# RWKV-7 rounds reordered: four-quarter products, sums with the identity on GpSimd

## The chip, the cores and the metric

The kernel runs on one core of a Trainium2 chip. The metric is the device time of one execution in microseconds (us); lower is better. TensorE (PE) multiplies into PSUM banks; VectorE (DVE), ScalarE (ACT) and GpSimd (POOL) work on SBUF tiles of 128 partitions; semaphores order them.

## The reference, cut to what matters

Two layers of a hybrid backbone over 256 context and 256 latent tokens. The change touches one mixer of layer 1, the bidirectional RWKV-7 with 16 heads of 64:

```python
def rwkv7_scan(r, w, k, v, a, b, state):
    def step(S, inp):
        r_t, w_t, k_t, v_t, a_t, b_t = inp
        sa = jnp.einsum('bhvk,bhk->bhv', S, a_t)
        S = S * w_t[:, :, None, :] + sa[..., None] * b_t[:, :, None, :] + v_t[..., None] * k_t[:, :, None, :]
        return S, jnp.einsum('bhvk,bhk->bhv', S, r_t)
...
        w_log = -jax.nn.softplus(-(rw_w0[d] + jnp.tanh(w_low[..., d, :]) @ rw_w2[d])) - 0.5
        a = jax.nn.sigmoid(rw_a0[d] + a_low[..., d, :] @ rw_a2[d])
        k_d = k * (1 + (a - 1) * rw_ka)
        out.append((r, exp(-exp(w_log)), k_d, v, -kk, kk * a))
```

It runs forward and backward (d = 0, 1), first over the context, then over the latent tokens.

## The kernel before, in words

The scan is done in chunks of L = 64 tokens, four of the context (seg 0, state only) and four of the latent tokens (seg 1, with outputs Y), both directions at once. `rwkv_chunks` makes nine calls of `rwkv_round(n, main, front)`: round n does the main part of chunk n-1 and the front part of chunk n. Each of TensorE, ACT, DVE and GpSimd has its own order, written out by hand in `pe_round`, `act_round`, `dve_round` and `pool_round`; a queue runs strictly in that order and waits on labels (`at_`, `at_last`).

Front: z (decay) and za (rate) by `low_rank`; `squashed` makes sigmoids of them by eight tanh and a rescale; `scan_decay` on DVE sums the decays; `decays` on ACT makes exponentials; from these come a, b, k, r of the next chunk, the products with ka, kk and k on GpSimd. Main: X = b'a is masked to D (inside blocks of 16 tokens) and, from Xt = a'b, to Dt and Ot (between blocks); T = (1+D)(1+D2)(1+D4)(1+D8) is built by adding a power times T to T on DVE (`add_power`); N = Ot T; U = (1 + N + N N + N N N) V1 is found by three steps V2, V3, U, each with a product and a sum on DVE (`substituted`). S is the state, S' = decay (S + bt U + kt vt).

A product of 64x64 matrices takes, for 8 head pairs p, halves hf and directions d, 32 matmuls of 64 rows by 64 columns. Tiles hold one head of a pair in partitions 0 to 63 and the other in 64 to 127. `half` says in which: tiles listed in `natural` are laid out alike for both directions, others with the halves exchanged for d = 1. A matmul whose input rows and output rows are both natural or both exchanged lies on the same quarter of the array for (d, hf) = (0, 0) and (1, 1) or its neighbour; with one natural and one exchanged the four positions are four different quarters. Before, products of two exchanged tiles are done one direction after the other (`each`); `both_wide` and `each_wide` take two right sides at once, into a pair of banks. Every product takes a PSUM bank out of four a direction, in turn, and waits until the bank's last user has read it (`bank_free`).

In the trace all products of one helper have one line: L2561 single products (`head`), L2579 and L2587 double width, L2602 turned tiles, L2610 z and za; L2744 ACT's copies, L2752 its tanh, L2739 other ACT steps; L379, L382 and L385 DVE multiply, add and subtract; L2922, L2923, L2926 and L2927 GpSimd.

## Time and profile before

| | |
|---|---|
| median of 3 runs | 2333.25 us (2330.16 to 2334.47) |
| profiled execution, span | 2316.3 us |
| changed stage (rounds 1 to 8) in it | 1447.0 to 1847.4 us |
| TensorE busy, whole span | 1964.1 us (85%) |
| DVE, ACT, GpSimd busy | 941.6, 702.3, 330.4 us |

The profile is of one execution; its span leaves out what lies before the first and behind the last instruction. "Busy" counts instructions of an engine, overlapping ones once; "issue" as the reason of an idle stretch means that the profile shows nothing for which the engine waited.

### The profile page before, as it was taken

How to read it: one execution, taken by the hardware profiler on the slowest of the kernel's cores; microseconds unless marked ns; L12 is line 12 of the kernel's file. 1: busy time of each engine (PE TensorE's matmuls, PEld its weight loads, DVE VectorE, ACT ScalarE, POOL GpSimd, SP SyncE). 2: the span in 40 equal slices, each digit the busy share in tenths (PEclk: the TensorE clock that was granted, in tenths of full speed). 3: DMA queues.
4: the chain of work that ended last, by engine and by line, in shares of the span. 5: the costliest groups of instructions: out<-in, count | busy, mean ns of one | idle time of the engine just before them, and what ended most of it. 6: DMA issues, size and time to landing. Idle time of an engine off the chain costs nothing. (4 is left out here: it accounts for less than half of the span.)

```text
span 2316.3 us, 58391 instructions
## 1 busy us (share of the span) xinstructions
PE 1964.1 (85%) x26021; PEld 1364.9 (59%) x26021; DVE 941.6 (41%) x1675; ACT 702.3 (30%) x1525; POOL 330.4 (14%) x211
## 2 busy tenths in 40 slices
PE   6999998997979888998487895888888897977775
PEld 3777765445844445555253685888878755633443
DVE  3183235785051111111434577666777453111112
ACT  3234534674230000100214344455444212000001
POOL 1433310002401000000110345212311000000000
PEclk8999999998989989999799997999999977988888
DMA  8554533204265789777530220000000025899975
GB/s 298 189 204 146 183 144 146 74 1 145 73 258 217 280 302 349 277 272 285 212 111 1 70 77 28 4 5 5 4 4 4 31 91 206 301 387 365 358 295 182
DMA packets 133329, 381.14 MB, mean 165 GB/s; under 512 B 14394, under 2 KB 43670, under 8 KB 115926
## 3 DMA queue, kind: packets, MB, share of 16 engines
q1 hardware_dynamic: 114528, 343.82, 40.3%
q10 hardware_dynamic: 15094, 20.99, 3.0%
q0 software_dynamic: 3456, 12.58, 1.4%
q8 instruction: 205, 3.36, 0.6%
q14 instruction: 46, 0.38, 0.0%
HBM read 634.54 MB, written 25.95 MB: 285 GB/s over the span
## 5 line engine op out<-in xcount | busy, mean ns | idle before, releaser
L371 PE MATMUL banks<-parts 128*128 128x512 f32 (+1 forms) x1096 | 244.7, 375 | 14.5 <-POOL parts L1523 7.6
L1814 PE MATMUL banks<-arena 128*32 128x256 f32 x1696 | 218.4, 403 | 40.8 <-DMA arena<-in_exp_w_up_dram 40.8
L371 PEld LDWEIGHTS banks<-parts 128*128 128x128 f32 x1096 | 194.6, 192 | 55.2 <-POOL parts L2388 9.4
L1815 PE MATMUL banks<-arena 128*32 128x256 f32 x1696 | 218.3, 402 | 0.0
L2561 PE MATMUL banks<-arena 64*64 64x64 f32 x4224 | 159.4, 225 | 47.7 <-DVE arena L382 18.5
L1880 ACT ACTIVATE arena<-banks 64x256 f32<-64x256 f32 x78 | 29.6, 380 | 549.9 <-PE banks L1815 382.6
L2561 PEld LDWEIGHTS banks<-arena 64*64 64x64 f32 x4224 | 147.7, 140 | 52.3 <-DVE arena L382 19.9
L1814 PEld LDWEIGHTS banks<-arena 128*32 128x32 f32 x1696 | 102.0, 115 | 120.5 <-DMA arena<-in_exp_w_up_dram 44.0
L371 PE MATMUL banks<-arena,ring 128*128 128x256 f32 (+2 forms) x560 | 163.3, 459 | 9.4 <-PEq L318 8.5
L2561 PE MATMUL banks<-ring 64*64 64x64 f32 x4224 | 159.9, 225 | 8.6 <-issue 7.4
L379 DVE TENSOR_TENSOR arena<-banks,arena 64x256 f32<-64x256 f32 (+3 forms) x128 | 65.5, 511 | 241.5 <-ACT arena L1880 149.9
L2005 DVE COPY arena<-banks 128x256 f32<-128x256 f32 x78 | 33.1, 425 | 309.1 <-DMA y_sorted<-arena 226.5
L2561 PEld LDWEIGHTS banks<-ring 64*64 64x64 f32 x4224 | 147.6, 139 | 10.3 <-issue 9.3
L1836 PE MATMUL banks<-arena 128*32 128x256 f32 x1696 | 114.5, 416 | 35.7 <-DVE arena L1995 18.4
L371 PEld LDWEIGHTS banks<-arena,ring 128*128 128x128 f32 (+1 forms) x560 | 108.7, 199 | 60.4 <-issue 46.8
L371 PE MATMUL banks<-h_parts,parts_z 128*128 128x512 f32 x416 | 132.0, 397 | 3.9 <-PEq L318 3.9
L2061 POOL DMA_INDIRECT arena<-y_sorted,slot_ids x12 | 12.0, 1000 | 743.9 <-DMA y_sorted<-arena 740.8
L2744 ACT ACTIVATE arena<-banks 128x512 f32<-128x512 f32 x88 | 52.4, 595 | 172.2 <-PE banks L2602 127.1
L1814 PE MATMUL banks<-ring,arena 128*32 128x256 f32 x800 | 100.0, 393 | 4.8 <-DMA ring<-in_exp_w_up_dram 4.8
L1836 PEld LDWEIGHTS banks<-arena 128*32 128x32 f32 x1696 | 55.9, 118 | 79.8 <-issue 27.3
L797 POOL TENSOR_TENSOR parts_z<-ring,parts_z 128x1024 fp32r<-128x1024 f32 x34 | 84.5, 2485 | 128.5 <-ACT parts_z L787 121.8
L1815 PEld LDWEIGHTS banks<-arena 128*32 128x32 f32 x1696 | 101.9, 115 | 0.0
(373 smaller groups left out, 3626.8 us busy)
## 6 DMA issues: line engine op xcount, KB each, us to landing
arena<-in_exp_w_gate_dram SPq DMA_DIRECT2D x106, 1024.0 KB
arena<-in_exp_w_up_dram SPq DMA_DIRECT2D x106, 1024.0 KB
arena<-in_exp_w_down_dram SPq DMA_DIRECT2D x53, 2048.0 KB
ring<-in_exp_w_gate_dram SPq DMA_DIRECT2D x50, 1024.0 KB
ring<-in_exp_w_up_dram SPq DMA_DIRECT2D x50, 1024.0 KB
ring<-in_exp_w_down_dram SPq DMA_DIRECT2D x25, 2048.0 KB
ring<-in_w_mod_dram SPq DMA_DIRECT2D x24, 2048.0 KB, 8.9
ring<-in_ab_w_in_dram SPq DMA_DIRECT2D x10, 2048.0 KB, 13.9
```

The source lines that it names most:

```text
L371: m = nc.tensor.matmul(o, a, b, start=first and n == 0, stop=last and n == len(pairs) - 1)
L379: return nc.vector.tensor_tensor(o, a, b, ALU.mult)
L797: nc.gpsimd.tensor_tensor(low, landed_part(j), whole(high), ALU.subtract).then_inc(pool_done, pool.tick(("w low", j), *((let_go(key),) if ...
L1814: nc.tensor.matmul(o[r:r + BLOCK, 0:256], x, up[:, k, c], start=k == 0, stop=k == KD - 1)
L1815: m = nc.tensor.matmul(o[64 + r:64 + r + BLOCK, 0:256], x, gate[:, k, c], start=k == 0, stop=k == KD - 1)
L1836: m = nc.tensor.matmul(ps[3 + i % 2][BLOCK * q:BLOCK * q + BLOCK, 0:256], x, w[:, k, 256 * q:256 * q + 256], start=k == 0, stop=k == 3)
L1880: nc.scalar.activation(m_sil[0:64, :], ps[i % 2][64:P, 0:256], ACT.Silu).then_inc(act_done, act.tick(("silu", i)))
L2005: nc.vector.tensor_copy(m_yout[:, (i - 1) % 2, :], ps[3 + (i - 1) % 2][:, 0:256]).then_inc(dve_done, dve.tick(("y out", i - 1)))
L2061: nc.gpsimd.indirect_dma_start(m_yg[:, t, a, :], None, y_sorted, bass.IndirectOffsetOnAxis(ap=slots[:, t, a:a + 1], axis=0)).then_inc(y_ga ...
L2561: m = nc.tensor.matmul(view(d, n_)[half(d, hf, n_), p, :], now[d][a][rows, p, :], now[d][b][rows, p, :], start=q == 0, stop=q == len(pairs ...
L2744: nc.scalar.activation(now[d]["W" if n_ == "W1" else n_], view(d, n_), ACT.Copy).then_inc(act_done, act.tick((n, n_, d), (n, n_ + " read", ...
```

## The change

The rounds are written anew. T is no longer a sum in place: T1 = 1 + D; T2 = K2 T1 with K2t = 1 + D2t, T4 = K4 T2 with K4t = 1 + D4t, and T8 = T4 + D8 T4. GpSimd makes K2t and K4t from ACT's copies of the powers, and KN = 1 + N from the copy of N (`with_one`). U = (1 + N2)(1 + N) V1 in two steps with N2 = N N, for which Nt is a product of its own. Natural and exchanged tiles alternate, so that D4, D4t, T2, D8t, T4, N, Nt, V1, N2 and V2 are done by `both`. The double-width products are gone. W and Y are opened in their bank by one product and completed in it by later ones (`opening`, `adding`), in place of sums on DVE. X, Xt and z of the next round are issued within this round (`pe_first`, `pe_second`, `pe_decay`), and so are their masks (`dve_first`, `dve_second`, `dve_third`). ACT copies one direction and DVE the other for T2, T4, W, V1 and V2. The rate's tanh is not rescaled: A Pinv = (tanh + 1) Pinv on DVE, and factors of 2 and 0.5 go into kinv, a, ka1, ka_half and ka2. b is multiplied on GpSimd instead of DVE, `A kk` is gone; Pinc is only made for seg 1.

```diff
+            s.update(b=s["A"], k=s["t"], T1=s["T"], T2=s["T"], T4=s["T"], T8=s["T"], K2t=s["W"])
+            s.update(D4=s["D"], D4t=s["Dt"], K4t=s["D2"], D8t=s["D2t"], N=s["D"], KN=s["Dt"], Nt=s["D2"], N2=s["Ot"],
+                     V1=s["D2t"], V2=s["D2"], U=s["D2"])
...
-        natural = ("a", "b", "k", "r", "S", "Y1", "Y", "z", "za")
+        natural = ("a", "b", "k", "r", "S", "Y", "z", "za", "D4", "D4t", "K4t", "T2", "N", "KN", "Nt", "V1")
...
+            four = (0, 0), (1, 1), (0, 1), (1, 0)
+
+            def head(n_, a, b, d, p, hf, start, stop):
+                rows = half(d, hf, a)
+                assert rows == half(d, hf, b)
+                return nc.tensor.matmul(view(d, n_)[half(d, hf, n_), p, :], now[d][a][rows, p, :], now[d][b][rows, p, :], start=start, stop=stop)
+
+            def both(n_, *pairs):
+
+                for p in range(8):
+                    for q, (a, b) in enumerate(pairs):
+                        for d, hf in four:
+                            m = head(n_, a, b, d, p, hf, q == 0, q == len(pairs) - 1)
+                m.then_inc(pe_done, pe.tick((n, n_ + " product", 0), (n, n_ + " product", 1)))
+
+            def opening(n_, a, b):
+
+                for p in range(8):
+                    for d, hf in four:
+                        m = head(n_, a, b, d, p, hf, p == 0, False)
+                m.then_inc(pe_done, pe.tick((n, n_ + " opened")))
+
+            def adding(n_, *pairs):
+
+                pe.wait_ge(*at_((n_ + " opened",)))
+                for p in range(8):
+                    for q, (a, b) in enumerate(pairs):
+                        for d, hf in four:
+                            m = head(n_, a, b, d, p, hf, False, p == 7 and q == len(pairs) - 1)
+                m.then_inc(pe_done, pe.tick((n, n_ + " product", 0), (n, n_ + " product", 1)))
+
...
+            def pe_first():
+                take("X", "D")
+                for d in range(2):
+                    from_last(d, "a", "b")
+                both("X", ("b", "a"))
+
+            def pe_second():
+                take("Xt", "Ot")
+                both("Xt", ("a", "b"))
...
+                following = rounds[n + 1] if front else None
+                if not main:
+                    pe_decay()
+                    take("AK")
+                        from_last(d, "k")
+                    both("AK", ("k", "a"))
+                    if seg == 1:
+                        take("RK")
+                        for d in range(2):
+                            from_last(d, "r")
+                        both("RK", ("k", "r"))
+                    take("D2")
+                        ready(d, "D", "Dt")
+                        each("D2", "Dt", "D", d)
+                    take("D2t")
+                    for d in range(2):
+                        each("D2t", "D", "Dt", d)
+                    if seg == 1:
+                        take("RB")
+                        both("RB", ("b", "r"))
+                    take("D4")
+                    for d in range(2):
+                        ready(d, "D2", "D2t")
+                    both("D4", ("D2t", "D2"))
+                    take("D4t")
+                    both("D4t", ("D2", "D2t"))
+                    take("T2")
+                    for d in range(2):
+                        ready(d, "K2t", "T1")
+                    both("T2", ("K2t", "T1"))
+                    take("bt")
+                    take("kt")
+                    take("za")
+                    take("D8t")
+                        ready(d, "D4", "D4t")
+                    both("D8t", ("D4", "D4t"))
+                    take("T4")
+                        ready(d, "K4t", "T2")
+                    both("T4", ("K4t", "T2"))
+                    take("vt")
+                    turned("vt", [chunk(b_v, seg, i, d) for d in range(2)])
+                    take("T8")
+                        ready(d, "D8t", "T4")
+                        each("T8", "D8t", "T4", d)
+                    take("W")
+                        ready(d, "AK", "vt")
+                    opening("W", "AK", "vt")
+                    take("N")
+                    for d in range(2):
+                        ready(d, "T8", "Ot")
+                    both("N", ("Ot", "T8"))
+                    for d in range(2):
+                        from_last(d, "S")
+                    adding("W", ("a", "S"))
+                    take("Nt")
+                    both("Nt", ("T8", "Ot"))
+                    take("V1")
+                    for d in range(2):
+                        ready(d, "W")
+                    both("V1", ("T8", "W"))
+                if front:
+                    following["pe first"]()
+                if main:
+                    take("N2")
+                    for d in range(2):
+                        ready(d, "N", "Nt")
+                    both("N2", ("Nt", "N"))
+                    take("V2")
+                    for d in range(2):
+                        ready(d, "KN", "V1")
+                    both("V2", ("KN", "V1"))
+                if front:
+                    following["pe second"]()
+                    take("Y")
+                    opening("Y", "S", "r")
+                if main:
+                    take("U")
+                        ready(d, "N2", "V2")
+                        each("U", "N2", "V2", d)
+                    if front and following["front"]:
+                        following["pe decay"]()
+                        ready(d, "U", "bt", "kt", "RB", "RK")
+                    if seg == 1:
+                        adding("Y", ("U", "RB"), ("vt", "RK"))
+                    take("S")
+                    both("S", ("bt", "U"), ("kt", "vt"))
+                elif following["front"]:
+                    following["pe decay"]()
...
                 if front:
                     for d in range(2):
-                        squashed("z", d, "sw", "sw", 0)
+                        squashed("z", d, "sw", 0)
+                        act.wait_ge(*at_(("tanh z", d)))
+                        fn(d, "sw", now[d]["sw"], now[d]["sw"], scale=0.5, bias=0.5)
                 if main:
+                    copied("D2")
+                    copied("D2t")
                     for d in range(2):
+                        act.wait_ge(*at_(("T1", d)))
+                    copied("D4")
+                    copied("D4t")
+                    copied("T2", (0,))
                 if front:
                     decays(0)
+                    decays(1)
                 if main:
+                    copied("bt")
+                    copied("kt")
+                if front:
                     for d in range(2):
+                        squashed("za", d, "A", 1)
                 if main:
+                    copied("D8t")
+                    copied("T4", (0,))
+                    copied("vt")
+                    copied("N")
+                    copied("W", (0,))
+                    copied("Nt")
+                    copied("V1", (0,))
+                    copied("N2")
+                    copied("V2", (0,))
+
...
+                def copied(n_, d=1):
+                    go(v.tensor_copy(now[d][n_], view(d, n_)), d, n_, n_ + " read")
+
+                def sum_of(n_, x, d):
+                    dve.wait_ge(*at_((x, d)))
+                    go(vadd(now[d][n_], now[d][x], view(d, n_)), d, n_, n_ + " read")
...
                 if main:
+                    if seg == 1:
+                        for d in range(2):
+                            masked("RB", "RB", d, 1, "RB read")
+                    copied("T2")
                 if front:
                     for d in range(2):
                         s = now[d]
                         dve.wait_ge(*at_(("Pexc", d)))
+                        go(v.scalar_tensor_tensor(s["next_a"], s["Pexc"], -2.0, chunk(b_kk, next_seg, j, d), ALU.mult, ALU.mult), d, "a")
+                        if next_seg == 1:
+                            dve.wait_ge(*at_(("Pinc", d)))
+                            go(vmul(s["next_r"], s["Pinc"], chunk(b_r, 1, j, d, NC_)), d, "r")
+                if main:
+                    copied("T4")
                     for d in range(2):
+                        sum_of("T8", "T4", d)
+                    copied("W")
                 if front:
                     for d in range(2):
                         s = now[d]
+                        dve.wait_ge(*at_(("A ka", d)))
+                        go(v.scalar_tensor_tensor(s["A"], s["A"], 1.0, s["Pinv"], ALU.add, ALU.mult), d, "A Pinv")
+                if main:
+                    copied("V1")
+                if front:
+                    following["dve first"]()
+                if main:
+                    copied("V2")
+                if front:
                     for d in range(2):
                         s = now[d]
                         dve.wait_ge(*at_(("t k", d)))
                         go(vmul(s["k"], s["t"], s["Pinv"]), d, "k")
+                    following["dve second"]()
+                if main:
+                    for d in range(2):
+                        sum_of("U", "V2", d)
+                if front:
+                    following["dve third"]()
+                if seg == 1:
+                    for d in range(2):
+                        dve.wait_ge(*at_(("Y product", d)))
+                        y = chunk(b_y, 1, i, d, NC_)
+                        go(vadd(y, y, view(d, "Y")), d, "Y read")
                 if main:
                     for d in range(2):
                         s = now[d]
                         end = s["end"].unsqueeze(2).to_broadcast([P, 8, L])
                         dve.wait_ge(*at_(("S product", d)))
+                        dve.wait_ge(*at_last(("next end", d)))
                         go(vadd(s["S"], s["S"], view(d, "S")), d, "S read")
                         go(vmul(s["S"], s["S"], end), d, "S")
...
+                def with_one(n_, source):
+                    for d in range(2):
+                        pool.wait_ge(*at_((source, d)))
+                        if n_ == "K4t":
+                            pool.wait_ge(*at_(("D4t product", d)))
+                        go(g(now[d][n_], now[d][source], one_of_heads, ALU.add), d, n_)
+
                 if main:
+                    with_one("K2t", "D2t")
+                    with_one("K4t", "D4t")
+                for d in range(2 if front else 0):
+                    s = now[d]
+                    pool.wait_ge(*at_(("tanh za", d)))
+                    go(g(s["t"], s["A"], across(ka_half), ALU.mult), d, "A ka")
+                for d in range(2 if front else 0):
+                    s = now[d]
+                    pool.wait_ge(*at_(("A Pinv", d)))
+                    go(g(s["b"], s["A"], chunk(b_kk, next_seg, j, d), ALU.mult), d, "b")
+                if main:
+                    with_one("KN", "N")
+                for d in range(2 if front else 0):
                     t = now[d]["t"]
                     go(g(t, t, across(ka1), ALU.add), d, "t")
                     go(g(t, t, chunk(b_k, next_seg, j, d), ALU.mult), d, "t k")
 
```

## Rows read from the trace of the kernel before

**Rows 1.** the page: span, TensorE's busy time, and its queue of code

```profile
span 2316.3 us, 58391 instructions
...
PE 1964.1 (85%) x26021; PEld 1364.9 (59%) x26021; DVE 941.6 (41%) x1675; ACT 702.3 (30%) x1525; POOL 330.4 (14%) x211
...
q8 instruction: 205, 3.36, 0.6%
```

**Rows 2.** busy time by stretch (us, busy and instructions of PE, PEld, DVE, ACT, POOL, clock)

```profile
1542.00:1588.00 46.00, 39.46 (x1528) 38.08 (x1523) 31.08 (x42) 24.39 (x64) 10.97 (x8) 1.00 0.02 4
1687.00:1741.00 54.00, 46.72 (x1785) 45.38 (x1785) 37.23 (x50) 24.77 (x64) 10.97 (x8) 0.97 0.02 4
```

**Rows 3.** TensorE's waits in the stage: line, releaser, us, times, longest

```profile
PE banks L2561 <- DVE arena L382: 18.5, 9, 2.4
PE banks L2561 <- DVE ring L379: 16.9, 1, 16.9
PE banks L2561 <- issue: 15.3, 17, 1.8
...
PE banks L2602 <- issue: 6.2, 6, 1.2
```

**Rows 4.** the timeline of PE: start, duration, instruction, idle time before it and releaser

```profile
1447.01 0.33 PE L2561 MATMUL banks<-arena 64*64 64x64 f32 x1 [16.94 <-DVE ring L379]
...
1485.27 0.51 PE L2561 MATMUL banks<-arena 64*64 64x64 f32 x10 [1.86 <-DVE arena L382]
...
1491.72 0.24 PE L2561 MATMUL banks<-arena 64*64 64x64 f32 x1 [0.96 <-DVE ring L382]
...
1495.02 0.21 PE L2561 MATMUL banks<-ring 64*64 64x64 f32 x1 [1.03 <-issue]
...
1498.39 0.27 PE L2579 MATMUL banks<-ring 64*64 64x128 f32 x1 [0.94 <-issue]
...
1501.73 0.21 PE L2561 MATMUL banks<-arena 64*64 64x64 f32 x1 [0.44 <-issue]
...
1686.89 0.21 PE L2561 MATMUL banks<-ring 64*64 64x64 f32 x1 [1.38 <-issue]
...
1690.36 0.21 PE L2602 MATMUL banks<-ident,arena 64*64 64x64 f32 x1 [1.22 <-issue]
...
1694.19 0.21 PE L2602 MATMUL banks<-ident,arena 64*64 64x64 f32 x1 [0.93 <-issue]
```

**Rows 5.** the DMA view of 1494 to 1512 us, in 40 slices

```profile
GB/s 0 0 0 0 36 0 0 0 0 0 0 0 36 0 0 0 0 0 0 0 36 0 0 0 0 0 0 36 0 0 0 0 0 0 0 36 0 0 0 0
```

**Rows 6.** TensorE in stretches of 3 us (length, busy, matmuls, granted clock)

```profile
1480.00:1483.00 3.00, 3.00 (x110) 1.00 0.02 5
1492.00:1495.00 3.00, 1.99 (x130) 1.00 0.02 5
1531.00:1534.00 3.00, 1.21 (x34) 0.93 0.00 0
1534.00:1537.00 3.00, 3.00 (x62) 0.50 0.03 5
```

**Rows 7.** the timeline of ACT: tanh of one direction, a copy of a product

```profile
1437.56 1.72 ACT L2752 ACTIVATE arena<-banks,arena 128x64 f32<-128x64 f32 x8
...
1458.59 0.60 ACT L2744 ACTIVATE ring<-banks 128x512 f32<-128x512 f32 x1 [0.34 <-PE banks L2561]
```

**Rows 8.** the timeline of GpSimd

```profile
1524.08 1.04 POOL L2922 TENSOR_TENSOR arena<-arena,vec 128x512 f32<-128x512 f32 x1 [36.00 <-ACT arena L2739]
...
1528.00 1.80 POOL L2923 TENSOR_TENSOR ring<-ring,arena 128x512 f32<-128x512 f32 x1
```

**Rows 9.** the timeline of DVE: a product beside GpSimd's, and the stage's end

```profile
1442.51 1.56 DVE L379 TENSOR_TENSOR arena<-arena 128x512 f32<-128x512 f32 x1 [3.84 <-POOL arena L2923]
...
1845.41 1.41 DVE L382 TENSOR_TENSOR arena<-arena,banks 128x512 f32<-128x512 f32 x2 [1.16 <-PE banks L2561]
1847.40 0.17 DVE L2998 TENSOR_SCALAR arena<-arena 128x8 f32<-128x8 f32 x1 [0.59 <-PEq L318]
```

More of the change, by code:

```diff
@@ new lines, in each, with turned @@
+            def each(n_, a, b, d):
+                for p in range(8):
+                    for hf in range(2):
+                        m = head(n_, a, b, d, p, hf, True, True)
+                m.then_inc(pe_done, pe.tick((n, n_ + " product", d)))
+            def turned(n_, x):
+                for p in range(8):
+                    for d, hf in four:
+                        rows = slice(64 * hf, 64 * hf + 64)
+                        m = nc.tensor.matmul(view(d, n_)[half(d, hf, n_), p, :], x[d][rows, p, :], ident[rows, rows], start=True, stop=True)
+                m.then_inc(pe_done, pe.tick((n, n_ + " product", 0), (n, n_ + " product", 1)))
@@ new lines, in low_rank @@
+            def low_rank(n_, w, x):
+                for p in range(8):
+                    for d, hf in four:
+                        rows, c = slice(64 * d, 64 * d + 64), first_column(next_seg, j, d)
+                        m = nc.tensor.matmul(view(d, n_)[64 * hf:64 * hf + 64, p, :], w[rows, p * P + 64 * hf:p * P + 64 * hf + 64],
+                                             x[rows, c:c + L], start=True, stop=True)
+                m.then_inc(pe_done, pe.tick((n, n_ + " product", 0), (n, n_ + " product", 1)))
@@ new lines, in masked, with dve_first @@
+            def masked(n_, source, d, k, *names):
+                dve.wait_ge(*at_((source + " product", d)))
+                go(vmul(now[d][n_], view(d, source), mask(d, k)), d, n_, *names)
+            one_of_heads = stackid[:].unsqueeze(1).to_broadcast([P, 8, L])
+            def dve_first():
+                for d in range(2):
+                    dve.wait_ge(*at_last(("N2 product", d)))
+                    dve.wait_ge(*at_last(("KN", d)))
+                    masked("D", "X", d, 2, "D read")
@@ L2802, in dve_round, with dve_second, dve_third @@
+            def dve_second():
+                for d in range(2):
+                    dve.wait_ge(*at_last(("V2 product", d)))
+                    masked("Dt", "Xt", d, 4)
+                for d in range(2):
+                    go(vadd(now[d]["T1"], now[d]["D"], one_of_heads), d, "T1")
+            def dve_third():
+                for d in range(2):
+                    dve.wait_ge(*at_last(("U product", d)))
+                    masked("Ot", "Xt", d, 5, "Ot read")
             def dve_round():
@@ L2803, in dve_round @@
                 v = nc.vector
-                def go(ins, d, *names):
-                    dve.step(ins, *[(n, n_, d) for n_ in names])
-                def mask(d, k):
-                    return b_rmask[:, d, k, :].unsqueeze(1).to_broadcast([P, 8, L])
-                def masked(n_, source, d, k, *names):
-                    dve.wait_ge(*at_((source + " product", d)))
-                    go(vmul(now[d][n_], view(d, source), mask(d, k)), d, n_, *names)
+                following = rounds[n + 1] if front else None
@@ L2847, in dve_round @@
                             masked("RK", "RK", d, 1, "RK read")
-                    for d in range(2):
-                        go(vadd(now[d]["T"], now[d]["D"], stackid[:].unsqueeze(1).to_broadcast([P, 8, L])), d, "T1")
-                    if seg == 1:
-                        for d in range(2):
-                            masked("RB", "RB", d, 1, "RB read")
-                    for d in range(2):
-                        add_power("T2", d)
                 if front:
@@ L2900, in dve_round @@
                         dve.wait_ge(*at_(("S product", d)))
+                        dve.wait_ge(*at_last(("next end", d)))
                         go(vadd(s["S"], s["S"], view(d, "S")), d, "S read")
                         go(vmul(s["S"], s["S"], end), d, "S")
-                    if seg == 1:
-                        for d in range(2):
-                            dve.wait_ge(*at_(("Y product", d)))
-                            y = chunk(b_y, 1, i, d, NC_)
-                            go(vadd(y, y, view(d, "Y")), d, "Y read")
             def pool_round():
@@ L2997, in dve_ @@
                 one = nc.vector.scalar_tensor_tensor
[L2998 removed]
+                dve.step(nc.vector.tensor_scalar(ka2, ka1, 4.0, -2.0, ALU.mult, ALU.add))
                 dve.wait_ge(*at("y root"))
```

323 lines of the change are left out of this document (49 added, 274 removed).

## The prediction

> **What bounds the kernel now.** I read first where in the span the changed code runs, then what TensorE does there, then what its idle time waits for, and last the queue that brings it its code. The changed stage runs from TensorE's first product of round 1 at 1447.01 us [rows 4] to 1847.36 us, where all engines start the next block: the first DVE instruction of that block stands at 1847.40 [rows 9]. That is 400.35 us for eight rounds, some 46.7 us for each of the four without outputs (seg 0) and 53.3 for each of the four with them (seg 1). Every other stage keeps its code, so the whole difference has to come from here or from the round ahead of it.
>
> In the stage no engine is full. In a round TensorE is busy 39.5 of 46 us, DVE 31.1, ACT 24.4, GpSimd 11.0 (seg 1: 46.7, 37.2, 24.8, 11.0 of 54) [rows 2]. 
>
> What TensorE waits for is the point. Its waits for DVE are few and large (16.9 us once, ahead of round 1, and 18.5 in nine), but 15.3 and 6.2 us are "issue", for nothing that the profile shows [rows 3]. In the timeline these stalls come in rows: 1495.02, 1498.39, 1501.73, and 1686.89, 1690.36, 1694.19 [rows 4]. Between two of them stand 125 to 128 visible matmuls, 250 to 256 instructions. The page has a queue of kind "instruction" with 205 packets and 3.36 MB, 16.4 KB each; TensorE's 2 x 26021 instructions [rows 1] over 205 are 254 each. In 18 us of the stage the DMA view shows five bursts of one packet's size, 3.15 to 3.6 us apart, and nothing else [rows 5]. So TensorE's code comes in **lines of 256 instructions, two sets each**, and the next but one is only asked for when a line is entered. A line of two four-quarter sets is done in 1.87 us and then stands until the fetch is over. Thirteen such spacings from stall to stall lie in the stage, from 3.34 to 4.00 us, mean 3.60 (the first and last of two runs are shown [rows 4]); without the two in which two-quarter work filled most of the line the mean is 3.55. I take **3.57 us a line**. No line is banked: TensorE idled 1.86 us before 1485.27 and 0.96 before 1491.72, had a slow stretch between them, and the next dense line stalls again at 1495.02 [rows 4].
>
> The Trainium skill, "Runtime: NRT & Kernel Launch", section "Instruction fetch mechanics", describes such 256-instruction blocks fetched while the one before runs, but says that the fetch is hidden, because the sequencer dispatches slower than the blocks arrive. By that page the stalls [rows 4] would not exist; this trace does not agree, and the sum goes by the trace. What that page would make of the time is the first rival.
>
> **The change, part by part.** *Number of sets.* Before: a seg 0 round has 23 sets (S counts two), a seg 1 round 27; 200 in the stage, 100 lines. After, by the new order of `pe_round`: 26 and 31 (X, Xt and z of the next round among them), the last round 27; 228 with round 0, of which 223 come from the first AK on: 111.5 lines. *Array time* falls all the same. Before, a seg 0 round is 7 four-quarter sets (6.5 us), two of double width (counted twice: 1.8 and 3.5) and 12 by `each` (22.4) and S (1.9): 36 us. After: 20 sets at 0.93, S 1.9, and two-quarter work only in D2, D2t, T8, U and in the opening of W (AK and vt lie in the same halves, so its four positions fall on two quarters): 5 x 1.87. Together 29 us; in seg 1 34.5 against 41. So 7 us a round leave the array, 55 in all. But the fetch takes 3.57 a line whatever the array does: 13 lines are 46.4 us, 15.5 are 55.3. The array's gain becomes stall, and 11.5 more lines have to come in. This is the step on which I place the forecast.
>
> *Lines longer than the fetch.* T8 with the opening of W, in seg 1 also D2 with D2t and Y's opening with U, are 3.74 us of array time: 0.17 over, about 14 times: +2.4 us.
>
> *GpSimd's adds* (K2t, K4t, KN: six in a round). GpSimd's tensor operations here take 1.04 to 1.80 us [rows 8], 14 a round against 8. K2t must be there for T2: D2t's half is copied 0.8 us after its end (ACT copy 0.60 plus 0.2 [rows 7]), two adds follow, 1.04 to 1.6 each: 4.9 us after D2t began, while D4 (0.85 waiting, 0.93) and D4t (0.93) end at 4.6; the 0.3 lies inside a line that stalls 1.7 anyway, so nothing. K4t has bt, kt, za and D8t ahead of T4: 7 us at line pace against 4, nothing.
>
> *ACT's queue.* Between T2 and T8 it has T2, the decays (2.7, four of 0.6 and two short), bt and kt (2.2), eight tanh a direction (1.72 [rows 7], 3.5 for both), D8t and T4: 10.8 us after T2's end. TensorE has six sets there, 10.7 us at line pace: met, without cover to spare.
>
> *The DVE and GpSimd chain at the round's end.* DVE's queue holds A Pinv behind W's copy, 2.8 us after the line of N and W begins. Then A Pinv 0.7, on GpSimd b x2, KN x2, t x2, t k x2 (10 us if each is at its short end, 13 at its long end, after [rows 8]; I take 11.3), k 0.7, Dt and T1 2.9, and U's sums 1.45, with S behind them: S starts 20 us after that line began. By lines S's comes at 5 x 3.57 = 17.9; it waits 2.1, runs 1.9, and so takes 4.0: 0.5 over the fetch. Four seg 0 rounds: +2 (0 if GpSimd is at its short end, +9 at its long). In seg 1 Y's opening adds a set ahead, and the wait lies within a stalling line: 0.
>
> *Start.* Round 0 has no sigmoid rescale of za and starts `A ka` on the tanh: X can start near 1444.4 instead of 1447.0 (tanh of za from 1437.0 at 1.72 a direction, A ka, A Pinv, two b of 1.3). But AK now comes first in the round and wants k, behind four more GpSimd operations (5.2 us) and a DVE multiply: k is there at about 1450.3, where before only the fourth set wanted it. X, Xt and z of round 1 are done by then. *End.* After the last set DVE has S's two adds and two multiplies, 4 x 0.72, where before it ended with 1.41 for Y [rows 9]: the block ends 3.4 us after the last set.
>
> **Sum:** 1450.3 + 111.5 x 3.57 (398.1) + 2.4 + 2 + 3.4 = 1856.2 against 1847.4: 8.8 us longer. The profiled execution has a span of 2316.3, 17 below the median of the runs, 2333.25; I carry the difference over: 2342. At 3.50 us a line it is +1, at 3.47 -2, at 3.65 +18.
>
> **Rivals.** *A: the fetch is no limit, or a cheaper one.* If code came for nothing, a round would last as long as its chain: 8.3 us to T2, 10.8 to T8, 5.6 to W, then 18 and S's 1.9: 44.6 in seg 0 and about 48.6 in seg 1 (RK, RB, the second decay, two more of Y), 2.1 and 4.7 less than now: -27, +3.3 at the start, +1.3 at the end: 2311. That is what the section of the Trainium skill cited above would lead to. If every fetch took 3.34 us, the shortest seen, it is 25.6 less than my sum: 2316. For it: a four-quarter product and long stretches without a wait. Against it: [rows 4, 5], and that the sets counted through lines give the old round (five to seven lines at the fetch, the wide and the two-quarter lines and the U chain above it: 46). *B: the end of the round becomes the bound.* DVE's operations between SBUF tiles take 1.56 us instead of 0.69 while GpSimd works [rows 9], and GpSimd now works nearly all the time that k, T1 and the sums are made. With GpSimd at 13 us and 2.6 more on DVE, S starts 24.3 us after the line of N: 4.5 us over in a seg 0 round, some 2.8 in a seg 1 round, 29 in place of 2: 2369. It decides from the point where GpSimd's eight operations and DVE's eight behind them pass 18 us. The clock can go with it: TensorE was busy 1.21 of 3 us, and the next three ran at a granted 0.50, 1.2 GHz [rows 6]. In a dense line that costs nothing (a set is then 1.66, two are 3.3, still under the fetch), at D2, T8 and U about 1 us each. *C, within the forecast:* the stalls are as before and everything cancels, within 5 us: that is 3.47 to 3.53 a line.
>
> **How the numbers follow.** Forecast case (fetch bound, -2 to +18) 0.60; rival A 0.15; rival B 0.25. The forecast case splits, by the mean of a line, into 0.05 faster by over 0.2%, 0.27 within it, 0.28 slower; B is slower nearly always (0.24, and 0.01 within), A faster. 0.2%, 4.7 us, is about what a measurement of this kernel can tell from no change. So faster 0.20, same 0.28, slower 0.52. The range reaches to the faster end of A at 3.34 us a line and most of B: 2316 to 2366.
>
> **What would show it.** In the changed kernel: some 219 packets of the instruction queue; "issue" as TensorE's largest wait in the stage, 100 us and more in place of 26, with stalls of 1.3 to 1.9 us every 128 matmuls, spaced 3.4 to 3.8; TensorE's busy time in the stage down by about 50 us with the stage as long as before. Against step "chain": waits for U's sum ahead of S over 3 us. Wrong would be the whole if the stalls were gone or the spacing in dense lines were well under 3.4.

## The result, and the profile after

The changed kernel takes 2366.96 us (median of 4 runs, 2362.11 to 2379.26) against 2331.7 for the kernel before on the same chips (4 runs, 2319.51 to 2334.47). The ratio is 1.0172, 95% interval 1.0136 to 1.0209: 1.4 to 2.1% slower. The forecast was 2342 with a range of 2316 to 2366: the sign was right, the size far too small. (In the later runs on other chips the kernel before had medians of 2325 to 2329, 7 to 17 runs each; against these it is 38 to 42 us more instead of 35.)

The page of the changed kernel, the same lines as [rows 1]:

```profile
span 2360.3 us, 62107 instructions
...
PE 1925.1 (82%) x27813; PEld 1321.0 (56%) x27813; DVE 902.3 (38%) x1612; ACT 708.0 (30%) x1557; POOL 389.8 (17%) x259
...
q8 instruction: 219, 3.59, 0.6%
```

TensorE has 1792 matmuls more and 39 us less busy time; the queue of code has 219 packets, 14 more, the number of the forecast. Busy time of one seg 0 and one seg 1 round (the columns of [rows 2]):

```profile
1553.00:1605.00 52.00, 34.40 (x1664) 32.20 (x1664) 26.49 (x33) 24.86 (x70) 18.49 (x14) 0.97 0.02 4
...
1770.00:1828.00 58.00, 39.18 (x1945) 36.94 (x1942) 29.19 (x38) 25.77 (x69) 18.28 (x14) 0.97 0.02 4
```

DVE is relieved by 4.6 and 8 us a round, TensorE by 5 and 7.5; the rounds last 52 and 58 us instead of 46 and 54. So nothing was gained where work went away, and the waits of TensorE in the stage (as [rows 3]) say what took its place:

```profile
PE banks L2545 <- issue: 89.9, 70, 2.1
PE banks L2545 <- POOL ring L2915: 20.3, 6, 15.0
PE banks L2582 <- issue: 20.2, 13, 2.0
PE banks L2545 <- DVE ring L382: 7.7, 7, 1.6
PE banks L2590 <- issue: 7.3, 6, 1.9
```

"issue" has grown from some 26 us to 117.4, TensorE's waits for the other engines in the stage have shrunk from 47 to 39, and its busy time from 343 to 305: together 46 of the 47 us by which the stage is longer. The timeline of TensorE (as [rows 4]) has the stalls in rows. These five are 3.35 to 4.02 us apart, with 127 visible matmuls from each to the next:

```profile
1670.76 0.27 PE L2545 MATMUL banks<-arena 64*64 64x64 f32 x1 [1.04 <-issue]
...
1674.66 0.21 PE L2545 MATMUL banks<-arena,scratch 64*64 64x64 f32 x1 [1.81 <-issue]
...
1678.68 0.21 PE L2582 MATMUL banks<-ident,ring 64*64 64x64 f32 x1 [1.88 <-issue]
...
1682.44 0.21 PE L2545 MATMUL banks<-ring 64*64 64x64 f32 x1 [1.67 <-issue]
...
1685.79 0.40 PE L2582 MATMUL banks<-ident,arena 64*64 64x64 f32 x12 [1.26 <-issue]
```

and the DMA view of 1676 to 1694 us has one packet of code for each (as [rows 5], 0.45 us a slice):

```profile
GB/s 0 0 0 0 0 0 0 0 36 0 0 0 0 0 0 0 36 0 0 0 0 0 0 0 36 0 0 0 0 0 0 0 36 0 0 0 0 0 0 0
```

Four packets in 18 us where [rows 5] had five. The whole kernel's time moves by up to 15 us from run to run in stages that the change doesn't touch (the changed stage begins at 1428 to 1443 us in the traces below), more than many an edit is worth. The comparisons therefore go by the length of the changed stage in each trace: from ACT's first tanh of round 0 to DVE's first instruction of the block behind it. It is 419.0 us before and 465.8 after, 46.8 longer. TensorE's first product of round 1 (X), AK and the next block came at

```profile
1445.33 0.34 PE L2545 MATMUL banks<-arena 64*64 64x64 f32 x1 [14.96 <-POOL ring L2915]
...
1451.55 0.24 PE L2545 MATMUL banks<-arena 64*64 64x64 f32 x1 [1.77 <-DVE ring L379]
...
1894.54 0.17 DVE L2995 TENSOR_SCALAR arena<-arena 128x8 f32<-128x8 f32 x1 [0.59 <-PEq L318]
```

### The profile page after: what moved, and what is told of

Its sections match the earlier page's. It is cut to its first block and busy times, and to the rows that moved or that the text cites. A ratio compares the mean times of both kernels' runs of the same rounds, so it can differ in the third digit from the quotient of the medians.

```text
span 2360.3 us, 62107 instructions
## 1 busy us (share of the span) xinstructions
PE 1925.1 (82%) x27813; PEld 1321.0 (56%) x27813; DVE 902.3 (38%) x1612; ACT 708.0 (30%) x1557; POOL 389.8 (17%) x259
## 3 DMA queue, kind: packets, MB, share of 16 engines
q1 hardware_dynamic: 114528, 343.82, 39.5%
## 5 line engine op out<-in xcount | busy, mean ns | idle before, releaser
L2545 PE MATMUL banks<-arena 64*64 64x64 f32 x5504 | 214.9, 229 | 80.0 <-issue 43.9
L2545 PEld LDWEIGHTS banks<-arena 64*64 64x64 f32 x5504 | 200.4, 143 | 90.7 <-issue 68.0
L2545 PE MATMUL banks<-ring 64*64 64x64 f32 x5504 | 215.3, 228 | 35.6 <-issue 35.5
L1814 PE MATMUL banks<-arena 128*32 128x256 f32 x1696 | 214.6, 397 | 35.6 <-DMA arena<-in_exp_w_up_dram 35.6
L2545 PEld LDWEIGHTS banks<-ring 64*64 64x64 f32 x5504 | 198.9, 142 | 39.0 <-issue 39.0
L1815 PE MATMUL banks<-arena 128*32 128x256 f32 x1696 | 214.6, 397 | 0.0
L1814 PEld LDWEIGHTS banks<-arena 128*32 128x32 f32 x1696 | 100.8, 114 | 113.4 <-DMA arena<-in_exp_w_up_dram 39.6
L1836 PE MATMUL banks<-arena 128*32 128x256 f32 x1696 | 116.0, 420 | 39.4 <-DVE arena L1995 21.4
L2721 ACT ACTIVATE arena<-banks 128x512 f32<-128x512 f32 x120 | 73.5, 615 | 175.7 <-PE banks L2545 165.1
L1814 PE MATMUL banks<-ring,arena 128*32 128x256 f32 x800 | 102.0, 399 | 5.0 <-DMA ring<-in_exp_w_up_dram 5.0
L1836 PEld LDWEIGHTS banks<-arena 128*32 128x32 f32 x1696 | 56.4, 119 | 83.8 <-issue 27.2
L1815 PE MATMUL banks<-ring,arena 128*32 128x256 f32 x800 | 101.8, 398 | 0.0
```

Of the source, the lines that this page charges most:

```text
L1814: nc.tensor.matmul(o[r:r + BLOCK, 0:256], x, up[:, k, c], start=k == 0, stop=k == KD - 1)
L1815: m = nc.tensor.matmul(o[64 + r:64 + r + BLOCK, 0:256], x, gate[:, k, c], start=k == 0, stop=k == KD - 1)
L1836: m = nc.tensor.matmul(ps[3 + i % 2][BLOCK * q:BLOCK * q + BLOCK, 0:256], x, w[:, k, 256 * q:256 * q + 256], start=k == 0, stop=k == 3)
L2545: return nc.tensor.matmul(view(d, n_)[half(d, hf, n_), p, :], now[d][a][rows, p, :], now[d][b][rows, p, :], start=start, stop=stop)
L2721: nc.scalar.activation(now[d][n_], view(d, n_), ACT.Copy).then_inc(act_done, act.tick((n, n_, d), (n, n_ + " read", d)))
```

## Experiments

| kernel | stage, us | code packets | stall to stall: mean us (number) | whole kernel, us (runs) |
|---|---|---|---|---|
| before | 419.0 | 205 | 3.60 (13) | see above |
| before again | 415.2 | 205 | 3.65 (14) | 2321.0 (1) |
| before, 64 instructions more | 416.6 | 205 | 3.65 (11) | 2326.35 (1) |
| before, bt twice | 432.1 | 209 | 3.77 (22) | 2331.28 (1) |
| before, z and za 64x128 | 419.2 | 201 | 3.76 (12) | 2328.93 (12) |
| changed | 465.8 | 219 | 3.81 (56) | 2366.96 (4) |
| changed again | 458.8 | 219 | 3.77 (55) | 2369.76 (1) |
| changed, 64 instructions more | 460.6 | 219 | 3.76 (57) | 2370.84 (1) |
| changed, bt twice | 478.8 | 223 | 3.75 (62) | 2385.85 (4) |
| changed, z and za 64x128 | 454.3 | 215 | 3.82 (47) | 2362.56 (4) |
| changed, A Pinv early | 455.8 | 219 | 3.80 (68) | 2363.98 (4) |
| changed, KN on DVE | 463.3 | 219 | 3.82 (64) | 2371.7 (1) |
| changed, three edits | 438.1 | 213 | 3.70 (44) | 2343.62 (6) |
| the same and KN on DVE | 442.5 | 213 | 3.74 (38) | 2357.27 (4) |
| changed, bf16 operands | 361.8 | 162 | | 2264.99 (2) |
| before, bf16 operands | 335.8 | 155 | | 2247.98 (2) |
| changed, bf16, A Pinv early | 335.5 | 162 | | 2240.98 (1) |

"Stall to stall" takes the pairs of issue stalls of 0.3 us and more that follow each other with no other wait between and 118 to 130 visible matmuls apart, one line of code. (The expectations below quote a narrower count: 3.56 to 3.61 before, 3.79 changed.) The stage of the same program differs by 4 to 7 us from trace to trace; what is below that is not told apart here. In what follows F is the theory that TensorE's code sets the pace, A that the array's time does, C that the chain of ACT, DVE and GpSimd does.

**More code, hardly any work.** The product bt is issued twice into its bank.

```diff
-                for p in range(8):
+                for again in range(2 if n_ == "bt" else 1):
+                  for p in range(8):
                     for d, hf in four:
```

> The changed kernel with the product bt issued twice in every round, into the same bank (64 more matmuls and weight loads a round, nothing else; the result is the same). Theory F, the stage is bound by the fetch of TensorE's code, 3.8 us for each line of 256 instructions: 8 sets more are 4 lines more, +15 us against the changed kernel, and 223 packets in the instruction queue instead of 219. Theory A, the array's time binds: +0.93 us a round, +7. Theory C, the chain of ACT, DVE and GpSimd binds: 0 to 1, since bt has 10 us of room before S wants it.

Measured: 223 packets and a stage of 478.8 us, 13 us over the changed kernel's first trace and 20 over its second; the whole kernel 2385.85, 19 over. TensorE's waits:

```profile
PE banks L2545 <- issue: 83.6, 71, 1.9
PE banks L2583 <- issue: 25.6, 17, 1.9
PE banks L2545 <- POOL ring L2916: 22.2, 7, 14.9
PE banks L2545 <- DVE ring L382: 10.6, 7, 3.1
```

TensorE is busy 6.6 us more, and its issue stalls stay at 116 us (117.4 and 105.6 in the two traces without the edit): the added sets did not fill the standing time. The size is F's 15; the array's time (7 us) and the chain (0 to 1) predict too little. Against the first trace the rest of the 13 us shows as waits for DVE and GpSimd, against the second mostly as issue, so this run alone doesn't say where it went. The kernel before got the same edit:

> The kernel before with the product bt issued twice in every round (4 lines more, array time +0.93 us a round). bt stands at the round's begin, where the stalls of the kernel before lie. F: the four lines cost 3.6 us each there, +14 us on a stage of 415 to 419, 209 packets. A: +7. If the kernel before has slack for code: 0 to 4.

Measured: 432.1 against 419.0 and 415.3, 13 to 17 us more for four lines, 209 packets. Here the issue stalls grew by 13.0 us, from 25.8 to 38.8, and TensorE's busy time by 3.1: code sets the pace at the beginning of the old rounds as well. Its whole time, 2331.28, is a single run, only 4.6 above the kernel before on that chip (2326.72, with runs from 2318 to 2334), and says nothing.

**Less code, but more array time.** z and za are made with 128 columns of weights at a time, one matmul where two stood. Both expectations take the array's time as unchanged.

```diff
-                    for d, hf in four:
+                    for d in range(2):
...
-                        m = nc.tensor.matmul(view(d, n_)[64 * hf:64 * hf + 64, p, :], w[rows, p * P + 64 * hf:p * P + 64 * hf + 64],
-                                             x[rows, c:c + L], start=True, stop=True)
+                        m = nc.tensor.matmul(view(d, n_)[:, p, :], w[rows, p * P:(p + 1) * P], x[rows, c:c + L], start=True, stop=True)
```

> The changed kernel with z and za made by 64x128 matmuls (one for both halves of a pair) instead of two of 64x64: half the instructions of these 16 sets, 4 lines fewer, at the same array time. F: -15 us against the changed kernel, 215 packets, the same spacing of the stalls. A: 0. C: 0.

Measured: 215 packets, stage 454.3: 11.5 below the first trace of the changed kernel, 4.5 below the second; in the whole kernel 4 us, with ranges that overlap. The array's time was not the same. One set of z in the changed kernel, and one with 128 columns (the columns of [rows 2], this product alone, PE and PEld):

```profile
1519.00:1521.00 2.00, 1.16 (x64) 1.05 (x64) 1.00 0.04 8
```

```profile
1577.00:1580.00 3.00, 2.00 (x32) 1.86 (x32) 1.00 0.02 5
```

From the first matmul's start to the last one's it is 0.98 us against 1.73, both at the full granted clock: half the instructions in nearly twice the time. TensorE's busy time in the stage rose from 305.3 to 320.6 us, while the issue stalls fell by 31 us, from 117.4 to 86.7. The stage got shorter although the array had more to do, which is F's sign and not A's; the size of F's 15 us is not reached.

> The kernel before with z and za made by 64x128 matmuls. F: 4 lines fewer, but before only part of the lines stood for the fetch (lines with two-quarter sets take 3.7 us of array time anyway): between -4 and -14 us against the kernel before. A and C: 0.

Measured: 201 packets, stage 419.2, whole kernel 2328.93 against 2328.69, ratio 0.9997 (0.9979 to 1.0015). Nothing: the expectation, 4 to 14 us less, missed. TensorE's busy time rose by 8.7 us (343.0 to 351.7) and its idle time fell by as much, 3.8 of it issue stalls. So this run can't tell how much four lines less are worth in the old rounds: the longer array time of the same edit took back what there was.

**The chain behind A Pinv.** A Pinv is taken out from behind W's copy.

```diff
                 if main:
                     copied("T4")
-                    for d in range(2):
-                        sum_of("T8", "T4", d)
-                    copied("W")
                 if front:
...
                         go(v.scalar_tensor_tensor(s["A"], s["A"], 1.0, s["Pinv"], ALU.add, ALU.mult), d, "A Pinv")
+                if main:
+                    for d in range(2):
+                        sum_of("T8", "T4", d)
+                    copied("W")
```

> The changed kernel with A Pinv taken in front of T8's sums in DVE's order (it stood behind W's copy); nothing else. GpSimd's eight operations behind it can start some 9 us earlier. C, as far as waits for b ahead of X and for U's sum ahead of S make lines longer than the fetch: the 20 us of waits for GpSimd less the 15 of the start, and most of 7.7 for DVE, go; -6 to -12 us. If the waits only fill time in which code was missing anyway: 0 to -2, with issue stalls growing by as much as the waits shrink.

Measured: stage 455.8, 10 below the first and 3 below the second trace of the changed kernel; whole kernel 3 below. The waits for b ahead of X are gone (only the start's 15.0 is left) and those for U's sum are down from 7.7 to 4.4, while issue grew by 7:

```profile
PE banks L2545 <- issue: 97.6, 76, 2.3
PE banks L2582 <- issue: 19.8, 13, 2.0
PE banks L2545 <- POOL ring L2916: 15.0, 1, 15.0
...
PE banks L2590 <- issue: 7.1, 6, 1.9
...
PE banks L2545 <- DVE ring L382: 4.4, 6, 0.9
```

So of the 8.6 us of waits that went, 7.1 came back as stalls for code, as the second branch of the expectation had it. What the edit is worth in the full kernel, 3 to 10 us by the trace that one compares with, is not told apart from nothing: the whole kernel's ranges overlap.

> The changed kernel with KN = 1 + N made by DVE from ACT's copy (0.69 us each, behind T8's sums) instead of by GpSimd (1.27 each, behind b). Only KN moves. C: GpSimd's queue behind b is 2.6 us shorter, so k, T1 and U's sum come earlier by as much and the wait for U's sum ahead of S (up to 1.6 us a round) goes: 2 to 5 us of the stage. F alone: 0. Stage 461 to 464 against 465.8, 219 packets.

```diff
+                    for d in range(2):
+                        dve.wait_ge(*at_(("N", d)))
+                        go(vadd(now[d]["KN"], now[d]["N"], one_of_heads), d, "KN")
...
-                if main:
-                    with_one("KN", "N")
```

Measured: 463.3, between the two traces of the changed kernel. Inconclusive; and added to the three edits below it gave no gain either, so no run shows that GpSimd's share in KN costs anything.

**All that helped.** AK and RK in seg 1 by `both_wide` of the kernel before, z and za by 128 columns, A Pinv early; then with KN on DVE.

> The changed kernel with three edits together: z and za by 64x128 matmuls (4 lines fewer), AK and RK in seg 1 as one product of double width with one load of k (2 lines fewer), A Pinv ahead of T8's sums. The profiles of the single edits gave -11.6 and -10.0 us for the stage (465.8 us in the changed kernel). F: these add up, with 2 x 3.8 = 7.6 more: stage 437, 213 packets, whole time some 29 below the changed kernel, still about 15 above the kernel before (111 lines against 100 would be 108 against 100). If the saved code only uncovers waits (C): stage 450 or more.

> The changed kernel with all that helped: z and za by 64x128 matmuls, AK and RK in double width, A Pinv ahead of T8's sums (stage 438.1 together) and KN on DVE. F: 213 lines of code stay, so the gain is only what is left of waits for GpSimd and DVE in the long lines, 0 to 4 us: stage 434 to 438, still 15 or more above the kernel before (415 to 419).

Measured: 213 packets, stage 438.1 where F had 437, whole kernel 2343.62, 23 us below the changed kernel where 29 were expected, and still slower than before: the ratio to the kernel before on the same chip is 1.0071 (1.004 to 1.0101). The 437 was added up from differences to the first, longer trace of the changed kernel, so that it was met so closely is in part luck. With KN on DVE the stage is 442.5 (434 to 438 expected) and the ratio 1.0147 (1.0112 to 1.0183): not better, by the whole kernel worse. No version of the new order with exact products beat the kernel before.

**Half the code.** The products read the upper halves of their fp32 operands as bf16: what is computed in the RWKV rounds is cut to bf16, and each matmul is one instruction with one weight load.

```diff
-                return nc.tensor.matmul(..., now[d][a][rows, p, :], now[d][b][rows, p, :], start=start, stop=stop)
+                return nc.tensor.matmul(..., low(now[d][a][rows, p, :]), low(now[d][b][rows, p, :]), start=start, stop=stop)
```

with `low(x)` = `x.bitcast(bfloat16)[..., 1::2]`, and likewise in `turned` and `low_rank`.

> The changed kernel whose RWKV products read the upper halves of their fp32 operands as bf16: each matmul is then one instruction with one weight load in place of two and two, so half the code of the stage, and a quarter or half of its array time; all waits, copies and sums are as they were. The numbers it computes are cut to bf16. F: 57 lines x 3.8 = 217 us are no bound any more, the stage falls from 466 to what the chain of ACT, DVE and GpSimd needs: 44.6 us a round less some 11 of array time, 8 x 34 + 25 = 295, at most 330. C (the chain binds in the full kernel): 466 less the array time on the chain, 11 to 15 a round, 350 to 380.

> The same edit in the kernel before: half the code, bf16 operands. If only code keeps the new order from its gain, the changed kernel with this edit is faster than this one, by 2 us a round or more (rival A's difference of chains, -23 us in all); if its chain is longer too, it is not. Here I expect a stage of 310 to 340 us.

Measured: 361.8 and 335.8. Both stages fall, by 80 to 104 us. In the changed kernel TensorE is busy 144 of 358 us, and the issue stalls are 17.7 us instead of 117.4: the bound of code is gone, and the next one is to be seen. It is the chain: TensorE waits 195 us for DVE, GpSimd and ACT, where it was 39. By its number alone, 361.8, the run would speak for C (350 to 380) and not for F (295 to 330); it is the stalls that speak for F, since C wanted the waits for the other engines to be there with the full code too. Code and array time were halved by the same edit, so the run doesn't part these two, as the runs with more code do; and the array ran at a granted 0.51, nearly all at the lower level of 1.2 GHz, all through the stage. In the changed kernel with bf16 the waits are

```profile
PE banks L2550 <- DVE ring L382: 54.2, 16, 7.5
PE banks L2550 <- POOL ring L2920: 35.3, 8, 16.2
PE banks L2550 <- ACT arena L2726: 26.4, 11, 4.1
...
PE banks L2550 <- issue: 14.9, 16, 1.8
```

and every round has one like this, S behind U's sum:

```profile
1538.57 0.23 PE L2550 MATMUL banks<-arena 64*64 64x64 bf16 x1 [7.37 <-DVE ring L382]
```

The old order with bf16 is 26 us shorter (granted clock 0.56). The new order's chain is not shorter than the old one's even when code is no bound.

> The changed kernel with bf16 operands (half the code; stage 361.8, TensorE waits 7.4 us for U's sum in each round) and with A Pinv ahead of T8's sums. The chain W copy, A Pinv, eight GpSimd operations, k, T1, U's sum is then begun earlier: if it is what sets the round once code is no bound, the 7 us wait shrinks to under 3 and the stage falls by 4 us a round or more, to 330 or less, level with the kernel before with the same operands (335.8). If another chain is next, it falls by under 10.

Measured, in one run: 335.5, 26 us less and level with the old order, as expected. The waits for b ahead of X went (the 35.3 for GpSimd became the start's 16.2, 19 us less). Those ahead of S, which should have shrunk to under 3 us, shrank from 7.2 to 5.4 on average over seven rounds, 13 us less; issue stalls rose by 11. So the place of A Pinv in DVE's queue was worth the whole difference between the orders, but less by the wait I named than by the one that I didn't.

**What a line costs.**

> The kernel before once more, for a second trace. My 3.57 us a line came from thirteen spacings of the first trace; the changed kernel shows 45 such with a mean of 3.79. If the fetch is slower in the changed kernel, this trace gives 3.5 to 3.6 again; if the first sample was just low, 3.7 to 3.8. Stage 419 us either way.

> The changed kernel once more, for a second trace: does its stage (465.8 us) and its line (3.79 us from stall to stall, 45 spacings) come out the same, or is a line's time a matter of the run? If of the run: another mean, 3.6 to 3.85, and a stage 112 times that difference away. If of the kernel: within 0.04 and 5 us.

```diff
-                for p in range(8):
+                for p in [0, 1, 2, 3][:4 * (n == 0 and n_ == "z")] + list(range(8)):
```

> The changed kernel with the first half of round 0's z product issued twice: 64 instructions more ahead of the stage's rounds, so that every border between lines of 256 falls 64 instructions earlier in the sets. If the line's time hangs on where the borders fall in the work (which waits stand behind a border), the mean moves by more than 0.05 and the stage by 5 us or more; if not, stage 465 to 468 as before and 3.75 to 3.83.

> The kernel before with the same 64 instructions more in round 0. Its four traces so far give 3.56, 3.61 (as it is), 3.75 and 3.74 (with z and za by 64x128 matmuls, with bt twice). If the borders' places matter: 3.7 or more and a stage some us over 419; if not: 3.55 to 3.65, stage 415 to 420.

Measured: the changed kernel's second trace has 3.77 and a stage of 458.8, with the borders moved 3.76 and 460.6; the kernel before 3.65, with the borders moved 3.65 too. The borders' places make no difference that shows. The kernel before as it stands stays a little lower (3.60 to 3.65, 38 spacings) than the changed one (3.76 to 3.81, 168), but with one product twice, or z wide, it too shows 3.77 and 3.76. A better measure takes every stall, not only neighbouring ones: the time from a stall's end to the next packet of code, and from a packet to the end of the stall that it ends. In the kernel before these are 1.21 and 2.49 us, in the changed kernel 1.35 and 2.46. That makes 3.70 and 3.81 a line, and 3.69 and 3.74 in the second traces. So 0.07 us a line and 7 us of stage are a matter of the run: the stage moved beyond the 5 us of the expectation, the count of neighbouring stalls by just its 0.04.

## Why the prediction was wrong in size and right in kind

**What bounds the stage: right.** Code comes in lines of 256 instructions, one line costs about 3.7 us if the work in it is shorter, lines are not banked. 219 packets were forecast and found. TensorE's busy time fell by 38 us from round 1 on (341.3 to 303.7), not by the 50 forecast, and none of it reached the end. Extra code with hardly any work cost 13 to 20 us for four lines in the new order and 13 to 17 in the old. In the forecast's list of array time the "20 sets at 0.93" are 19 (with 20 there would be 27 sets in a round); its sum of 29 us has the 19. The rows give 34.4 us for such a round (39.5 before, where the list has 36): the list is short by 3 to 6 us a round, before and after, which costs nothing where code is the limit.

**The price of a line: mis-sized.** This is the first step that failed. The forecast took 3.57 us, between the 3.60 that is the mean of thirteen spacings, which scatter by 0.2, and the 3.55 that is left without the two longest. In the first trace of the changed kernel, 98 of the 111 spacings between packets from AK's line on are up to 4.25 us, with a mean of 3.78. Over 111.5 lines that is 23 of the 38.3 us by which the stage's end was missed (1894.5 against 1856.2). The trace of before held a better number, 3.70, in the distances between stalls and packets, which use every stall; it would have given 14.5 of them. What remains, up to 0.1 us a line between runs and orders, has no cause that the runs show.

**Lines longer than their fetch: mis-sized.** This is the second step that failed. I had 4.4 us for them (2.4 for two-quarter work, 2 for waits). In the trace the other 13 spacings, those above 4.25 us, are together 15.0 over 3.78: 10.6 more than forecast. In the second trace, where the short spacings have a mean of 3.67, it is the other way round: 12 us by the price and 15 by the long lines. Eight of the 13 lie in two places. One is S behind U's sum, with waits of 0.5 to 1.6 us, which the forecast had priced at 2 us in all; the other is one that it doesn't name, X behind b:

```profile
1539.77 0.24 PE L2545 MATMUL banks<-arena 64*64 64x64 f32 x1 [1.23 <-POOL ring L2915]
...
1553.04 0.24 PE L2545 MATMUL banks<-arena 64*64 64x64 f32 x1 [1.36 <-DVE ring L382]
```

Around the first, the timelines of DVE and GpSimd show where b's delay came from:

```profile
1535.02 0.69 DVE L2820 COPY arena<-banks 128x512 f32<-128x512 f32 x1 [5.25 <-PE banks L2545]
1535.74 0.69 DVE L2857 SCALAR_TENSOR_TENSOR arena<-arena 128x512 f32<-128x512 f32 x1
```

```profile
1524.28 1.04 POOL L2911 TENSOR_TENSOR ring<-ring,arena 128x512 f32<-128x512 f32 x1 [0.59 <-ACT ring L2727]
1536.58 1.70 POOL L2915 TENSOR_TENSOR arena<-arena 128x512 f32<-128x512 f32 x1 [11.25 <-DVE arena L2857]
1538.36 1.27 POOL L2915 TENSOR_TENSOR ring<-ring,arena 128x512 f32<-128x512 f32 x1
```

A Pinv (L2857) had its input at 1525.3 and stood ten us behind W's copy, GpSimd idle for 11.25. The forecast saw that queue and priced only what came behind it, up to U's sum, and not b's delay ahead of X.

**Start and end: right.** X came at 1445.33 (1444.4 forecast), AK at 1451.55 (1450.3), and the next block 3.6 us after the last set (3.4).

**From the stage to the whole kernel: luck.** The stage's end was missed by 38.3 us and the median only by 25. The forecast carried over 17 us from the profiled span before to the median before. For the changed kernel these are only 6.7 us apart (2360.3 and 2366.96), and what follows the stage took 3 us less in its trace than in the one before (465.8 against 468.9), in code that the change doesn't touch. Both are chance: four runs of the changed kernel lie 17 us apart, and its second trace has 469.9.

**The rivals.** A, that code is no limit or cheaper, is refuted, and so is its claim that the new order's chain is shorter: with half the code it is 26 us longer until A Pinv is moved. The section "Instruction fetch mechanics" of the Trainium skill's page "Runtime: NRT & Kernel Launch", by which the fetch is hidden behind the sequencer's pace, does not hold in this stage, where matmuls are short and four run at once: 117 us of stalls. B gave the measured time (2369) almost exactly, but mostly not by its mechanism: all waits ahead of S are 7.7 us in the new trace, where it wanted some 29. That its number fits is luck: the time was that of the forecast's own mechanism with a dearer line and the start of B.

## What to carry to other kernels

There, a change that empties the array but adds instructions loses, as this one did. Fewer and wider instructions can pay even at a price: with 128 columns of weights z's sets took nearly twice their array time, and the code-bound stage still got 4 to 12 us shorter. In the kernel before, where TensorE stalls less for code, the same edit gained nothing. A price that multiplies a hundred times needs all the samples of the trace, not the clean ones.

## What was not expected of the hardware

With bf16 operands TensorE was busy 144 of 358 us and its granted clock stayed at 0.51 for the whole stage, while in the fp32 rounds, with 89 issue stalls of 1.3 us on average, it was busy 304 of 458 us and kept 0.94. Two matmuls with 64 rows and 128 columns of weights, one on each half of the rows, start 7 ns apart, but the next pair starts some 0.11 us later: 32 of them took 1.73 us, where 64 matmuls with 64 columns took 0.98. And the same product order costs 3.74 to 3.81 us a line by run, with single spacings of packets from 3.3 us up, while the queues carried nothing but code: 109 packets of TensorE's and 7 of another instruction queue between 1465 and 1890 us.
